# The last product pair of each seven-product group in another order and on other PSUM banks, and the group's first product copied earlier

## The chip, the cores and the metric

The kernel runs on one core of a Trainium2 chip. The metric is the device time of one execution in microseconds (us). Three runs of the kernel before gave 2209.78, 2209.79 and 2210.81 us, median 2209.79.

## What is computed

One inference step of a two-layer backbone (width 1024, 128 context and 512 latent tokens, side by side as 640 columns). The part that matters here is the dense products:

```python
h = RMSNorm(x) * (1 + scale1) + shift1
qkv... = h @ w_in                      # column groups for four mixers
x += gate1 * (sum(gates * up) @ w_o)
h2 = RMSNorm(x) * (1 + scale2) + shift2
a, b = split(h2 @ w_ffn_in)            # w_ffn_in: 1024 x 5632
x += gate2 * ((silu(a) * b) @ w_ffn_out)
```

Everything is float32. Each number is split into a high and a low part, and a product is the sum high*high + high*low + low*high, so three matmuls stand for one.

## The kernel before

Activations lie transposed, 128 channels by 640 token columns, in two halves of 320. A *unit* is a 128x128 piece of weights; `product` (line 755) runs it against both halves, 6 matmuls of 128x320. A *chunk* is one block of 128 output channels: 8 units for an inner width of 1024, 48 matmuls. Two PSUM tensors take the chunks in turn, `lp[0]` for s=0 and `lp[1]` for s=1; each has two banks, `[:, 0]` and `[:, 1]`, one per half. After a chunk DVE or ACT reads the tensor out and counts up `drained[s]`; the next chunk of the same s waits for that. Weights arrive from HBM in `wst[:, s]`, ACT writes their high part to `wr[:, s, 0]` (`weight_hi`), DVE the low part to `wr[:, s, 1]` (`weight_lo`), which counts up `w_lo[s]`.

Part of the in-projection and most of the first feed-forward matrix go another way. A pair of chunks (256 output channels, 1024 inputs, 640 columns) is taken as a 2x2 by 2x2 block product with seven products, P1 to P7, instead of eight (Strassen's scheme in Winograd's form). One product is 12 matmuls of 128x320 (line 1011). There are four groups of such pairs per layer: FAST_IN (6 pairs, 42 products), FAST_A (5 pairs, 35), FAST_B and FAST_C (7 pairs, 49 each), so eight groups in two layers. `ring_order` gives the order: P1 of the first pair, and then for every pair P2, P6, P7, P5, then P1 of the next pair, then P3, P4. In the last pair no P1 stands between P5 and P3.

The seven products use one bank A of their own (P1, then P6, P5 and P3 added on top of it, `bank`) and two shared banks: P2 in `lp[0][:, 1]`, P7 and P4 in `lp[1][:, 1]`. A is `lp[m % 2][:, 0]` for pair m. In between, A is read out: ACT copies it after P1 (`p1_out`) and after P6 (`u2_out`), DVE adds it after P5 (`c22_out`, line 1891), and ACT reads it after P3 (`c12_out`, line 1347). DVE reads P2 (`c11_out`, line 1887) and P4 (`c21_out`, line 1899). P3 waits for `c22_out`, P4 for `p7_out`, P6 for `p1_out`.

The weights of the seven products (operands) are sums and differences of the raw weight blocks. They go through a ring of six places in `wr`: places 0 to 2 lie in `wr[:, 0]`, places 3 to 5 in `wr[:, 1]`. ACT writes the high part (`fast_hi`, line 1315), DVE the low part (`fast_lo`, line 1862, counts up `op_lo`). An operand can be written when the product that used its place before is done: operand i is written around product i-5. One exception is made by `ring_places`: where the last operand of a group would fall on place 0, it takes place 3, so that places 0 to 2 come free for the weights of the next stage:

```python
    places = [i % RING for i in range(n)]
    if places[-1] == 0:
        places[-1] = RING // 2
```

This holds for the groups of 49 products (operand 48, counted from 0), not for those of 42 and 35. The product that had place 3 before is number 45, so operand 48 is written only after it: high part behind product 45 (P7), low part behind product 46 (P5, after the `c22_out` add).

Behind FAST_A, FAST_B and FAST_C come the chunks of `w_ffn_out` (`outward`, eight chunks of 8, 7 and 7 units). Their first weights are loaded into the place of the raw weight blocks, by SP, in this order:

```python
for s in range(2):
    sy.wait_ge(op_lo, nth_op(l, g, FAST[g] - 1, (P3, P4)[s]))
    weight(l, out, src, 0, s)
```

`op_lo` counts operands in the order of the products, so "P3" here means all operands up to and with P3 of the last pair. ACT writes the high part of the first (`out_first_hi`, line 1367) in its step for the third-last product, and DVE the low part (`weight_lo`, line 1623) in its step for the second-last one; both take their steps in the order of the products. Before the first chunk PE waits for `c11_out`, `c12_out` and `c21_out` of the last pair. In layer 1, groups FAST_A and FAST_B, a `modulate_half` (small matmuls, line 1022) stands behind P4 of each of the last four pairs.

At the start of FAST_B and FAST_C the last chunk of the stage before (s=1) has just ended in `lp[1]`, and DVE reads it out in `residual` (line 1643, three instructions); before FAST_A it is the last chunk of the plain feed-forward pairs, read out by DVE at line 2102. P1 of the first pair waits for `drained[0]`, P2 too, and P7 (fourth product) for `drained[1]`. ACT writes operands 3, 4 and 5 there, and then copies P1.

Of the kernel before, what the change touches and what calls it, by code (L numbers as in the profile page):

```python
# [26 lines left out]
P = 128  # L27
DM = 1024
KD = DM // P
# [54 lines left out]
def ring_order(pairs):  # L84

    order = [(0, P1)]
    for m in range(pairs):
        order += [(m, P2), (m, P6), (m, P7), (m, P5)]
        if m + 1 < pairs:
            order.append((m + 1, P1))  # L90
        order += [(m, P3), (m, P4)]
    return order


ORDER = [ring_order(n) for n in FAST]
# [124 lines left out]
def build(nc, xT, ada, adb, win, wgu, wo, wff, wfa, wfb, vec, cond, fgv, cst, rope, dft, bias, ckT, cvt,  # L220
          yT, okT, ovt):
    with ExitStack() as ctx:
# [190 lines left out]
        def pairs_before(l, g, m):  # L413

            return l * FAST0[4] + FAST0[g] + m
# [44 lines left out]
                return H[:, low, HALF_K + k, TH:T]  # L460
            return turned_block(g, {P5: 1, P6: 2, P7: 3, P4: 4}[which], low)[:, k, :]

        def bank(m, which):

            if which in (P2, P7, P4):
                return lp[0 if which == P2 else 1][:, 1, 0:TH]
            return lp[m % 2][:, 0, 0:TH]

        def chunks_of(g, m):

# [279 lines left out]
        def _(pe):  # L750
# [43 lines left out]
            def weights(l, stage, j, s):  # L794
                pe.wait_ge(w_lo[s], 1 + l * PER_SLOT + SLOT0[stage] // 2 + j + 1)

            def fill(l, p, place):

                for n, k in FILL.get((p, place), ()):
                    s = n % 2  # L800
                    if k < KD:
                        if k == 0:
                            weights(l, GATE, n // 2, s)
                            pe.wait_ge(drained[0], gate0(l) + n)
                        mm = product(lp[0], weight_unit(s, k), H, k, k == 0, k == KD - 1)
                        if k == KD - 1:
                            mm.then_inc(lin[0], 1)
                    else:
                        if k == KD:
# [161 lines left out]
            def fast_product(l, g, i):  # L971

                m, which = ORDER[g][i]
                n = pairs_before(l, g, m)
                pe.wait_ge(op_lo, nth_op(l, g, m, which))
                if which == P1:
                    if m >= 2:
                        pe.wait_ge(c12_out, n - 1)
                    else:
                        pe.wait_ge(drained[m], 1 + l * PER_DR + D0[AHEAD[g]])  # L980
                if which == P2:
                    if m:
                        pe.wait_ge(c11_out, n)
                    else:
                        pe.wait_ge(drained[0], 1 + l * PER_DR + D0[AHEAD[g]])
                if which == P7:
                    if m:
                        pe.wait_ge(c21_out, n)
                    else:
                        pe.wait_ge(drained[1], 1 + l * PER_DR + D0[AHEAD[g]])  # L990
                new_blocks = g <= FAST_A and m == 0
                if which == P6:
                    pe.wait_ge(p1_out, n + 1)
                    if new_blocks:
                        pe.wait_ge(t_lo, turned_set(l, g) + 1)
                if which == P7 and new_blocks:
                    pe.wait_ge(t_lo, turned_set(l, g) + 2)
                if which == P5:
                    pe.wait_ge(u2_out, n + 1)
                    if new_blocks:  # L1000
                        pe.wait_ge(t_lo, turned_set(l, g) + 4)
                if which == P3:
                    pe.wait_ge(c22_out, n + 1)
                if which == P4:
                    pe.wait_ge(p7_out, n + 1)
                    if new_blocks:
                        pe.wait_ge(t_lo, turned_set(l, g) + 3)
                fresh = which in (P1, P2, P7)
                for k in range(HALF_K):
                    for j, (wi, ai) in enumerate(((0, 0), (0, 1), (1, 0))):  # L1010
                        mm = pe.matmul(bank(m, which), operand(g, i, wi)[:, k * P:(k + 1) * P], passing(g, which, ai, k),  # L1011
                                       start=fresh and k == 0 and j == 0, stop=k == HALF_K - 1 and j == 2,
                                       skip_group_check=not fresh)
                mm.then_inc(prod, 1)
# [12 lines left out]
            for l in range(L):  # L1027
# [65 lines left out]
                for i, (m, which) in enumerate(ORDER[FAST_IN]):  # L1093
                    fast_product(l, FAST_IN, i)
                    c0, c1 = chunks_of(FAST_IN, m)
                    if which == P2 and m:
                        turn_chunk(c0 - 1)
                    if which == P7 and turn_at(l, c0) is not None:
                        turn_of(c0, turn_at(l, c0))()
                    if which == P4:  # L1100
                        turn_chunk(c0)
                        if c1 < 4 * len(groups_in(l)):
                            quad_in(0)
                            modulate(ss[0], four(sm), c1 // 2 % 2)
# [4 lines left out]
                for c in range(2):  # L1109
# [9 lines left out]
                for out_of in (c11_out, c12_out, c21_out):  # L1119
                    pe.wait_ge(out_of, pairs_before(l, FAST_IN, FAST[FAST_IN]))  # L1120
                fill(l, 0, "f")


# [51 lines left out]
                for g, inner in zip(FF_GROUPS, (S_GA, S_GB, S_GC)):  # L1175
# [10 lines left out]

                    def outward(j, ready=None):
                        for s in range(2):
                            weights(l, out, j, s)
                            chunk(l, out, j, s, G_by_half, range(UNITS[out]), ready=None if s else ready)  # L1190

                    pe.wait_ge(c11_out, pairs_before(l, g, FAST[g]))
                    pe.wait_ge(c12_out, pairs_before(l, g, FAST[g]))
                    pe.wait_ge(c21_out, pairs_before(l, g, FAST[g]))
                    outward(0, inner)
                    with pe.Fori(1, KD // 2 - 1) as j:
                        outward(j)
# [9 lines left out]
        def _(act):  # L1207
# [93 lines left out]
            def fast_hi(l, g, i):  # L1301
# [12 lines left out]
                    act.wait_ge(w_sum, 4 * n + {P5: 1, P7: 2, P6: 3, P3: 4}[which])  # L1314
                act.activation(operand(g, i, 0), source(m, which), ACT.Copy).then_inc(op_hi, 1)  # L1315

            def fast_step(l, g, i):

                m, which = ORDER[g][i]
                n = pairs_before(l, g, m)  # L1320
                A, t1, inner = bank(m, P1), tmp[:, 1, :], g != FAST_IN
                a, b = [product_to(g, m, part) for part in range(2)]
                act.wait_ge(prod, OPS * pairs_before(l, g, 0) + i + 1)
                if which == P1:
                    if n:
                        act.wait_ge(c11_out, n)
                    if g == FAST_A and m == 0:
                        act.wait_ge(split, l * PER_SPL + SP0[S_GA] + 2)
                    act.activation(t1[:, 0:TH], A, ACT.Copy).then_inc(p1_out, 1)
                if which == P6:  # L1330
                    if n:
                        act.wait_ge(c21_out, n)
# [1 line left out]
                if which == P7:  # L1334
                    if inner:
                        act.wait_ge(hid, hid_before(l, g, m))
                    elif turned_before(l, g, m, 1) is not None:
                        act.wait_ge(turned, turned_before(l, g, m, 1))
                    elif chunks_of(g, m)[1] == IN_A + NV_TM:
                        act.wait_ge(op_lo, nth_op(l, g, m, P5))  # L1340
                    act.activation(b[:, TH:T], bank(m, P7), ACT.Copy).then_inc(p7_out, 1)
# [72 lines left out]
            for l in range(L):  # L1414
# [21 lines left out]
                for c in range(2 * PLAIN):  # L1436
# [13 lines left out]
                    if c == 2 * PLAIN - 2:  # L1450
                        for o in range(RING // 2):
                            fast_hi(l, FAST_IN, o)
                for o in range(RING // 2, RING):
                    fast_hi(l, FAST_IN, o)
                for i, (m, which) in enumerate(ORDER[FAST_IN]):
                    fast_step(l, FAST_IN, i)
# [93 lines left out]
                for g in FF_GROUPS:  # L1550
                    out = AHEAD[g]
                    if g > FAST_A:
                        for o in range(RING // 2):
                            fast_hi(l, g, o)
                    for o in range(RING // 2, RING):
                        fast_hi(l, g, o)
                    for i in range(OPS * FAST[g]):
                        fast_step(l, g, i)
# [17 lines left out]
        def _(ve):  # L1576
# [297 lines left out]
            def fast_step(l, g, i):  # L1874
# [5 lines left out]
                if which == P2:  # L1880
# [6 lines left out]
                    ve.tensor_tensor(a[:, 0:TH], tmp[:, 1, 0:TH], bank(m, P2), ALU.add).then_inc(c11_out, 1)  # L1887
                if which == P5:
                    ve.wait_ge(prod, first + i + 1)
                    ve.wait_ge(p7_out, n + 1)  # L1890
                    ve.tensor_tensor(b[:, TH:T], b[:, TH:T], bank(m, P5), ALU.add).then_inc(c22_out, 1)  # L1891
                if which == P4:
                    ve.wait_ge(u2_out, n + 1)
                    ve.wait_ge(prod, first + i + 1)
# [4 lines left out]
                    ve.tensor_tensor(b[:, 0:TH], tmp[:, 1, TH:T], bank(m, P4), ALU.add).then_inc(c21_out, 1)  # L1899
# [370 lines left out]
```

## Time and profile before

| | |
|---|---|
| three runs, median | 2209.79 us |
| profiled execution, time | 2210.49 us |
| its span, first to last instruction | 2208.7 us |
| PE busy | 2143.6 us, 97% of the span |
| DVE busy, ACT busy | 1310.0 us (59%), 900.9 us (41%) |
| matmuls of the seven-product groups (line 1011) | 4200 (2256 + 1368 + 288 + 144 + 96 + 48) |
| mean granted TensorE clock | 0.991 |
| HBM | 101 GB/s over the span |

The profiled execution takes 2210.49 us, 1.8 us more than its span, and lies 0.7 us above the median. Times in the rows below are microseconds from the start of the span. In a timeline row the first number is the start, the second the length of the merged piece, `x12` the number of instructions in it; the bracket gives the engine's idle time before it and what ended it. A piece of matmuls is some 0.15 us longer than the distance to the next piece, because the last matmul overlaps the next one.

### The profile page before, as it was taken

Reading aid. Unit: us, or ns where it says so; the run is one execution under the profiler, and the core shown is the slowest. Engines: PE = TensorE matmul, PEld = TensorE weight load, DVE = VectorE, ACT = ScalarE, POOL = GpSimd, SP = SyncE. Lnnn points to the kernel's source line nnn. Section 1 sums busy time; section 2 is a strip of 40 time slices with the busy share of each in tenths; the row PEclk is TensorE's granted clock in tenths of the full one; section 3 lists DMA queues with packets and bytes.
Section 4 is the critical chain, followed back from the end, with each engine's and each line's share of the span. In section 5 each row is a group of like instructions: output and inputs, shape, how many; then the busy total and the mean of one; then the engine's idle time right before and its main releaser. Section 6 shows DMA issues by size and latency. Waiting matters only on the chain. (4 is left out here: it accounts for less than half of the span.)

```text
span 2208.7 us, 38208 instructions
## 1 busy us (share of the span) xinstructions
PE 2143.6 (97%) x15247; PEld 2018.2 (91%) x15247; DVE 1310.0 (59%) x2493; ACT 900.9 (41%) x1574; POOL 0.2 (0%) x4
## 2 busy tenths in 40 slices
PE   8999999999999999999999999999999999999997
PEld 6998887888998999999989988888899899999997
DVE  5665656665447737558456565566644575474764
ACT  4533444443326415325344334444433364252441
POOL 0000000000000000000000000000000000000000
PEclk9999999999999999999989999999999999999999
DMA  8633321112341422322444233111124232222222
GB/s 295 226 134 109 117 77 49 49 49 72 100 148 61 152 89 92 127 89 77 153 172 161 91 124 118 57 49 49 49 89 156 66 96 68 86 77 72 92 72 81
DMA packets 70774, 225.81 MB, mean 102 GB/s; under 512 B 6992, under 2 KB 13776, under 8 KB 70480
## 3 DMA queue, kind: packets, MB, share of 16 engines
q1 hardware_dynamic: 70608, 223.50, 30.2%
q8 instruction: 116, 1.90, 0.3%
q14 instruction: 50, 0.41, 0.1%
HBM read 215.48 MB, written 6.55 MB: 101 GB/s over the span
## 5 line engine op out<-in xcount | busy, mean ns | idle before, releaser
L755 PE MATMUL lp<-H,wr 128*128 128x320 f32 x4800 | 769.2, 314 | 11.3 <-DVE H L1601 5.1
L755 PEld LDWEIGHTS lp<-H,wr 128*128 128x128 f32 x4800 | 712.4, 189 | 38.2 <-issue 25.5
L1011 PE MATMUL lp<-H,wr 128*128 128x320 f32 x2256 | 350.7, 310 | 5.4 <-DVE tmp L1891 4.0
L1011 PEld LDWEIGHTS lp<-H,wr 128*128 128x128 f32 x2256 | 334.2, 188 | 12.2 <-issue 11.4
L755 PEld LDWEIGHTS lp<-G,wr 128*128 128x128 f32 x2112 | 309.8, 188 | 5.4 <-issue 5.4
L755 PE MATMUL lp<-G,wr 128*128 128x320 f32 x2112 | 311.5, 309 | 3.2 <-issue 3.2
L1229 ACT ACTIVATE wr<-wst 128x1280 fp32r<-128x1280 f32 (+2 forms) x136 | 153.5, 1129 | 179.0 <-PE lp L755 178.3
L1623 DVE TENSOR_TENSOR wr<-wst,wr 128x1280 fp32r<-128x1280 f32 (+2 forms) x152 | 198.4, 1306 | 41.7 <-ACT wr L1229 36.1
L1011 PE MATMUL lp<-TT,wr 128*128 128x320 f32 x1368 | 213.1, 308 | 2.1 <-issue 2.1
L1315 ACT ACTIVATE wr<-wst 128x512 fp32r<-128x512 f32 x256 | 159.6, 627 | 127.4 <-PE lp L1011 75.3
L1011 PEld LDWEIGHTS lp<-TT,wr 128*128 128x128 f32 x1368 | 203.7, 188 | 2.5 <-issue 2.5
L1643 DVE SCALAR_TENSOR_TENSOR x<-lp,mod,x 128x128 f32 (+3 forms) x192 | 72.6, 434 | 201.5 <-PE lp L755 201.5
L1862 DVE TENSOR_TENSOR wr<-wst,wr 128x512 fp32r<-128x512 f32 x256 | 173.7, 685 | 9.1 <-ACT wr L1315 8.9
L755 PE MATMUL lp<-BR,wr 128*128 128x320 f32 x960 | 161.3, 313 | 1.8 <-DVE tmp L1680 1.8
L755 PEld LDWEIGHTS lp<-BR,wr 128*128 128x128 f32 x960 | 143.2, 188 | 8.1 <-issue 3.8
L1271 ACT ACTIVATE prob<-ss,st 128x640 f32<-128x640 f32 (+1 forms) x88 | 59.7, 679 | 132.3 <-DVE st L1722 130.9
L1271 ACT ACTIVATE prob<-sp,st 128x640 f32<-128x640 f32 (+3 forms) x72 | 51.4, 714 | 130.6 <-DVE st L1718 119.7
L1250 ACT ACTIVATE tmp<-lp,vc 128x640 f32<-128x640 f32 x64 | 50.7, 792 | 120.9 <-PE lp L755 120.9
L1283 ACT ACTIVATE pts<-ss 128x640 f32<-128x640 f32 (+3 forms) x120 | 64.4, 570 | 65.2 <-PE ss L912 43.0
L1721 DVE TENSOR_REDUCE st<-ss 128x1 f32<-128x640 f32 (+1 forms) x88 | 59.4, 675 | 50.4 <-PE ss L885 37.8
L1518 ACT ACTIVATE tmp<-x 128x640 f32 (+1 forms) x32 | 23.6, 739 | 159.9 <-DVE x L1643 159.9
L1680 DVE SCALAR_TENSOR_TENSOR tmp<-tmp,lp 128x640 f32<-128x640 f32 x48 | 39.2, 816 | 69.6 <-PE lp L755 69.3
(200 smaller groups left out, 2125.4 us busy)
## 6 DMA issues: line engine op xcount, KB each, us to landing
wst<-wgu SPq DMA_DIRECT2D x64, 640.0 KB, 3.9
wst<-wff SPq DMA_DIRECT2D x72, 512.0 KB, 3.6
sm<-adb SPq DMA_DIRECT2D x13, 2048.0 KB, 8.5
wst<-win SPq DMA_DIRECT2D x30, 512.0 KB, 4.5
wst<-wfb SPq DMA_DIRECT2D x32, 448.0 KB, 3.3
bt<-bias SPq DMA_DIRECT2D x32, 320.0 KB, 3.3
adae<-adb SPq DMA_DIRECT2D x8, 1024.0 KB, 15.0
wst<-wo SPq DMA_DIRECT2D x16, 512.0 KB, 3.7
```

Of the source, the lines that this page charges most:

```text
L755: mm = pe.matmul(out[:, h, 0:TH], w[wi], act[:, ai, k, h * TH:(h + 1) * TH], start=first and i == 0, stop=last and i == 2)
L1011: mm = pe.matmul(bank(m, which), operand(g, i, wi)[:, k * P:(k + 1) * P], passing(g, which, ai, k), start=fresh and k == 0 and j == 0, sto ...
L1229: act.activation(wr[:, s, 0, 0:w], wst[:, s, 0:w], ACT.Copy).then_inc(w_hi[s], 1)
L1250: act.activation(halves(tmp[:, 2 + n % 2, :]), lp[0][:, :, 0:TH], ACT.Tanh, bias=vc[:, i:i + 1], scale=0.5).then_inc(drained[0], 1)
L1271: act.activation(prob[:, u, lo:hi], src, ACT.Exp, bias=nm[:, q:q + 1], scale=SC_DIFF if kind == "df" else 1.0, accum_out=rs[:, q:q + 1]).t ...
L1283: act.activation(pts[:, f % 2, lo:KEYS], sflat[u][:, lo:KEYS], ACT.Copy).then_inc(pt_out, 1)
L1315: act.activation(operand(g, i, 0), source(m, which), ACT.Copy).then_inc(op_hi, 1)
L1623: ve.tensor_tensor(wr[:, s, 1, 0:w], wst[:, s, 0:w], wr[:, s, 0, 0:w].bitcast(F32), ALU.subtract).then_inc(w_lo[s], 1)
L1643: m = ve.scalar_tensor_tensor(out=x[:, k, a:b], in0=lp[s][:, h, a - h * TH:b - h * TH], scalar=mod[:, gate + 2 * j + s, c:c + 1], in1=x[:, ...
L1680: ve.scalar_tensor_tensor(out=halves(mg[:, kd, :] if first else tmp[:, 1, :]), in0=gate, scalar=1.0, in1=up, op0=ALU.add, op1=ALU.mult).th ...
L1721: own.step(ve.tensor_reduce(mx, S[:, at_:at_ + KEYS - lo], AX.X, ALU.max))
L1862: ve.tensor_tensor(operand(g, i, 1), source(m, which), operand(g, i, 0).bitcast(F32), ALU.subtract).then_inc(op_lo, 1)
```

## The change

The order of the last pair of every group becomes P2, P6, P7, P5, P4, P3. Bank A of pair m becomes `lp[(FAST[g] - m) % 2][:, 0]`, so that the last pair always has A in `lp[1]`; for the groups of 35 and 49 products this turns all banks A round, and the first pair has A in `lp[1]` as well. P1 of the first two pairs waits for `drained` of its own bank. The wait ahead of the next stage is split: the chunk in `lp[0]` waits for `c11_out` of the last pair and `c12_out` of the pair before, the chunk in `lp[1]` for `c12_out` and `c21_out` of the last pair. ACT copies the group's first product behind operand 3, ahead of operands 4 and 5. In FAST_IN the transposes of the last pair's first chunk (`turn_chunk`) move behind P3, which is now the last product. `ring_places`, SP's code, and the steps of `out_first_hi` and `weight_lo` stay as they are.

```diff
@@ ring_order
         order += [(m, P2), (m, P6), (m, P7), (m, P5)]
         if m + 1 < pairs:
-            order.append((m + 1, P1))
-        order += [(m, P3), (m, P4)]
-    return order
+            order += [(m + 1, P1), (m, P3), (m, P4)]
+    return order + [(pairs - 1, P4), (pairs - 1, P3)]
...
+        def first_bank(g, m):
+            return (FAST[g] - m) % 2
...
             if which in (P2, P7, P4):
                 return lp[0 if which == P2 else 1][:, 1, 0:TH]
-            return lp[m % 2][:, 0, 0:TH]
+            return lp[first_bank(g, m)][:, 0, 0:TH]
@@ PE
+            def first_bank_free(l, g):
+                pe.wait_ge(c11_out, pairs_before(l, g, FAST[g]))
+                pe.wait_ge(c12_out, pairs_before(l, g, FAST[g] - 1))
+            def second_bank_free(l, g):
+                pe.wait_ge(c12_out, pairs_before(l, g, FAST[g]))
+                pe.wait_ge(c21_out, pairs_before(l, g, FAST[g]))
...
-                        pe.wait_ge(drained[m], 1 + l * PER_DR + D0[AHEAD[g]])
+                        pe.wait_ge(drained[first_bank(g, m)], 1 + l * PER_DR + D0[AHEAD[g]])
...
-                    if which == P4:
+                    if which == (P3 if m == FAST[FAST_IN] - 1 else P4):
                         turn_chunk(c0)
...
                         for s in range(2):
+                            if isinstance(j, int) and j == 0:
+                                (second_bank_free if s else first_bank_free)(l, g)
                             weights(l, out, j, s)
...
-                    pe.wait_ge(c11_out, pairs_before(l, g, FAST[g]))
-                    pe.wait_ge(c12_out, pairs_before(l, g, FAST[g]))
-                    pe.wait_ge(c21_out, pairs_before(l, g, FAST[g]))
                     outward(0, inner)
@@ ACT
-                for o in range(RING // 2, RING):
+                fast_hi(l, FAST_IN, RING // 2)
+                first_product_out(l, FAST_IN, 0)
+                for o in range(RING // 2 + 1, RING):
                     fast_hi(l, FAST_IN, o)
...
-                    for o in range(RING // 2, RING):
+                    fast_hi(l, g, RING // 2)
+                    first_product_out(l, g, 0)
+                    for o in range(RING // 2 + 1, RING):
                         fast_hi(l, g, o)
```

`first_product_out` is the copy that stood in ACT's step for P1, with the same waits. The three places below show how the instructions move. In the rows `lp0` and `lp1` are the two PSUM tensors, `H` and `TT` the activation blocks, `G` the inner activations of the feed-forward part; the bracket names the semaphores that the instruction waits for.

PE, end of FAST_B in layer 1, from P5 to the first chunk behind the group, before:

```order
L1011 MATMUL lp0<-H_52,wr_89 128x320 [waits u2_out,op_lo]
L1011 MATMUL lp0<-H_52,wr_89 128x320 x11
L1011 MATMUL lp0<-H_52,wr_89 128x320 [waits c22_out,op_lo]
L1011 MATMUL lp0<-H_52,wr_89 128x320 x11
L1011 MATMUL lp1<-TT_56,wr_89 128x320 [waits p7_out,op_lo]
L1011 MATMUL lp1<-TT_56,wr_89 128x320 x11
L1022 MATMUL ss0<-sm2_57,cds_91 32x256 [waits ld_h]
L1022 MATMUL ss0<-sm2_57,cds_91 32x256 x7
L755 MATMUL lp0<-G_55,wr_89 128x320 [waits w_lo0,drained0,c21_out,split,c12_out,c11_out]
```

The same place in the change:

```order
L1026 MATMUL lp1<-H_52,wr_89 128x320 [waits u2_out,op_lo]
L1026 MATMUL lp1<-H_52,wr_89 128x320 x11
L1026 MATMUL lp1<-TT_56,wr_89 128x320 [waits p7_out,op_lo]
L1026 MATMUL lp1<-TT_56,wr_89 128x320 x11
L1037 MATMUL ss0<-sm2_57,cds_91 32x256 [waits ld_h]
L1037 MATMUL ss0<-sm2_57,cds_91 32x256 x7
L1026 MATMUL lp1<-H_52,wr_89 128x320 [waits c22_out,op_lo]
L1026 MATMUL lp1<-H_52,wr_89 128x320 x11
L758 MATMUL lp0<-G_55,wr_89 128x320 [waits drained0,w_lo0,split,c12_out,c11_out]
```

P4 and the small matmuls now stand between P5 and P3, and the first chunk no longer waits for `c21_out`.

DVE, the same end of FAST_B, before (line 1891 reads P5, 1862 writes operand 48, 1623 the low part of the next stage's first weights, 1899 reads P4):

```order
L1891 TENSOR_TENSOR tmp_87<-tmp_87,lp0 128x320 [waits p7_out,prod]
L1862 TENSOR_TENSOR wr_89<-wst_88,wr_89 128x512 [waits op_hi]
L1623 TENSOR_TENSOR wr_89<-wst_88,wr_89 128x896 [waits w_hi0]
L1899 TENSOR_TENSOR tmp_87<-tmp_87,lp1 128x320 [waits prod,u2_out]
L1919 TENSOR_TENSOR tmp_87<-tmp_87 128x640 [waits c22_out,c21_out,split,c12_out,c11_silu]
```

In the change:

```order
L1915 TENSOR_TENSOR tmp_87<-tmp_87,lp1 128x320 [waits p7_out,prod]
L1886 TENSOR_TENSOR wr_89<-wst_88,wr_89 128x512 [waits op_hi]
L1923 TENSOR_TENSOR tmp_87<-tmp_87,lp1 128x320 [waits prod,u2_out]
L1647 TENSOR_TENSOR wr_89<-wst_88,wr_89 128x896 [waits w_hi0]
L1943 TENSOR_TENSOR tmp_87<-tmp_87 128x640 [waits c22_out,c21_out,split,c12_out,c11_silu]
```

The weights' low part now stands behind the read of P4. Operand 48, in the second row, was P4's and is now P3's.

PE, start of FAST_B in layer 1, the last chunk before it and P1, P2 and P6, before:

```order
L755 MATMUL lp1<-G_55,wr_89 128x320 x47
L1011 MATMUL lp0<-H_52,wr_89 128x320 [waits drained0,op_lo]
L1011 MATMUL lp0<-H_52,wr_89 128x320 x11
L1011 MATMUL lp0<-H_52,wr_89 128x320 [waits drained0,op_lo]
L1011 MATMUL lp0<-H_52,wr_89 128x320 x11
L1011 MATMUL lp0<-TT_56,wr_89 128x320 [waits p1_out,op_lo]
```

In the change:

```order
L758 MATMUL lp1<-G_55,wr_89 128x320 x47
L1026 MATMUL lp1<-H_52,wr_89 128x320 [waits drained1,op_lo]
L1026 MATMUL lp1<-H_52,wr_89 128x320 x11
L1026 MATMUL lp0<-H_52,wr_89 128x320 [waits drained0,op_lo]
L1026 MATMUL lp0<-H_52,wr_89 128x320 x11
L1026 MATMUL lp1<-TT_56,wr_89 128x320 [waits p1_out,op_lo]
```

P1 now goes to the tensor that the chunk directly ahead of it has filled, and waits for `drained1`.

## Rows read from the trace of the kernel before

**Rows 1.** Waits of PE: whom it waited for, total us, times, longest us.

```profile
PE lp L1011 <- DVE tmp L1891: 4.0, 6, 0.7
PE lp L1011 <- DVE qk L1891: 1.3, 2, 0.7
PE lp L755 <- issue: 3.2, 4, 0.8
```

**Rows 2.** Timeline, end of FAST_B in layer 2.

```profile
1996.53 20.37 SPq L553 DMA_DIRECT2D wst<-wfb  x5
...
2000.42 1.92 PE L1011 MATMUL lp<-H,wr 128*128 128x320 f32 x12
...
2002.38 0.95 ACT L1367 ACTIVATE wr<-wst 128x896 fp32r<-128x896 f32 x1 [0.80 <-PE lp L1011]
...
2002.79 0.68 DVE L1862 TENSOR_TENSOR wr<-wst,wr 128x512 fp32r<-128x512 f32 x1
...
2003.02 2.00 PE L1011 MATMUL lp<-H,wr 128*128 128x320 f32 x12 [0.67 <-DVE tmp L1891]
2003.39 1.09 DVE L1623 TENSOR_TENSOR wr<-wst,wr 128x896 fp32r<-128x896 f32 x1
...
2007.58 12.70 PE L755 MATMUL lp<-G,wr 128*128 128x320 f32 x85 [0.80 <-issue]
```

**Rows 3.** Timeline, start of FAST_B in layer 2.

```profile
1919.46 3.68 PE L1011 MATMUL lp<-H,wr 128*128 128x320 f32 x24
...
1919.67 1.13 DVE L1643 SCALAR_TENSOR_TENSOR x<-lp,mod,x 128x128 f32<-128x128 f32 x3 [1.20 <-PE lp L755]
```

**Rows 4.** DMA issues near Rows 2: two loads, KB each, us to landing.

```profile
wst<-wfb SPq DMA_DIRECT2D x1, 448.0 KB, 3.4
...
wst<-wfb SPq DMA_DIRECT2D x1, 448.0 KB, 4.1
```

**Rows 5.** Timeline, end of FAST_A in layer 2, ends of FAST_A and FAST_B in layer 1.

```profile
1859.05 1.23 DVE L1623 TENSOR_TENSOR wr<-wst,wr 128x1024 fp32r<-128x1024 f32 x1 [0.69 <-ACT wr L1367]
...
1862.37 0.49 DVE L1899 TENSOR_TENSOR tmp<-tmp,lp 128x320 f32<-128x320 f32 x1 [2.10 <-PE lp L1011]
...
777.95 1.07 PE L1022 MATMUL ss<-sm,cds 128*32 128x256 f32 x16
...
923.12 0.68 DVE L1862 TENSOR_TENSOR wr<-wst,wr 128x512 fp32r<-128x512 f32 x1
...
928.04 12.15 PE L755 MATMUL lp<-G,wr 128*128 128x320 f32 x81
```

**Rows 6.** Timeline, start of FAST_A in layer 2.

```profile
1798.25 3.77 PE L1011 MATMUL lp<-H,wr 128*128 128x320 f32 x24
1798.31 0.82 DVE L2102 TENSOR_TENSOR tmp<-lp,tmp 128x640 f32<-128x640 f32 x1 [2.85 <-PE lp L755]
...
1800.98 0.61 ACT L1315 ACTIVATE wr<-wst 128x512 fp32r<-128x512 f32 x1
...
1802.54 0.41 ACT L1329 ACTIVATE tmp<-lp 128x320 f32<-128x320 f32 x1
...
1803.05 3.75 PE L1011 MATMUL lp<-TT,wr 128*128 128x320 f32 x24 [1.03 <-issue]
```

**Rows 7.** PE's longest idle times early in the mixers of each layer, and the block behind the first (timeline).

```profile
198.18 0.49 PE L898 MATMUL ss<-qk 64*128 64x128 f32 x4 [2.21 <-DVE ofm L1769]
198.60 3.10 PE L755 MATMUL lp<-H,wr 128*128 128x320 f32 x12
...
1286.92 0.49 PE L898 MATMUL ss<-qk 64*128 64x128 f32 x4 [1.58 <-DVE ofm L1769]
```

**Rows 8.** Stretches of PE: length, busy (matmuls), granted clock, DMA share, GB/s.

```profile
199.00:199.50 0.50, 0.50 (x5) 0.69 0.00 0
...
202.50:203.00 0.50, 0.50 (x5) 0.90 0.00 0
...
2002.00:2008.00 6.00, 4.52 (x30) 1.00 0.46 148
```

More of the change, by code:

```diff
@@ L461, in passing, with bank @@
             return turned_block(g, {P5: 1, P6: 2, P7: 3, P4: 4}[which], low)[:, k, :]
-        def bank(m, which):
+        def first_bank(g, m):
+            return (FAST[g] - m) % 2
+        def bank(g, m, which):
             if which in (P2, P7, P4):
                 return lp[0 if which == P2 else 1][:, 1, 0:TH]
-            return lp[m % 2][:, 0, 0:TH]
+            return lp[first_bank(g, m)][:, 0, 0:TH]
         def chunks_of(g, m):
@@ L808, in fill @@
                     else:
+                        if (n, k) == (0, KD):
+                            second_bank_free(l, FAST_IN)
                         if k == KD:
@@ L1010, in fast_product @@
                     for j, (wi, ai) in enumerate(((0, 0), (0, 1), (1, 0))):
-                        mm = pe.matmul(bank(m, which), operand(g, i, wi)[:, k * P:(k + 1) * P], passing(g, which, ai, k),
+                        mm = pe.matmul(bank(g, m, which), operand(g, i, wi)[:, k * P:(k + 1) * P], passing(g, which, ai, k),
                                        start=fresh and k == 0 and j == 0, stop=k == HALF_K - 1 and j == 2,
@@ L1118, in _ @@
                     mm.then_inc(f1, 1)
-                for out_of in (c11_out, c12_out, c21_out):
-                    pe.wait_ge(out_of, pairs_before(l, FAST_IN, FAST[FAST_IN]))
+                first_bank_free(l, FAST_IN)
                 fill(l, 0, "f")
@@ L1315, in fast_hi, with first_product_out @@
                 act.activation(operand(g, i, 0), source(m, which), ACT.Copy).then_inc(op_hi, 1)
+            def first_product_out(l, g, m):
+                n = pairs_before(l, g, m)
+                act.wait_ge(prod, OPS * pairs_before(l, g, 0) + PLACE[g][m, P1] + 1)
+                if n:
+                    act.wait_ge(c11_out, n)
+                if g == FAST_A and m == 0:
+                    act.wait_ge(split, l * PER_SPL + SP0[S_GA] + 2)
+                act.activation(tmp[:, 1, 0:TH], bank(g, m, P1), ACT.Copy).then_inc(p1_out, 1)
             def fast_step(l, g, i):
@@ L1320, in fast_step @@
                 n = pairs_before(l, g, m)
-                A, t1, inner = bank(m, P1), tmp[:, 1, :], g != FAST_IN
+                A, t1, inner = bank(g, m, P1), tmp[:, 1, :], g != FAST_IN
                 a, b = [product_to(g, m, part) for part in range(2)]
@@ L1324, in fast_step @@
                 if which == P1:
[L1325 to L1329, printed above, removed]
+                    if m:
+                        first_product_out(l, g, m)
                 if which == P6:
@@ L1340, in fast_step @@
                         act.wait_ge(op_lo, nth_op(l, g, m, P5))
-                    act.activation(b[:, TH:T], bank(m, P7), ACT.Copy).then_inc(p7_out, 1)
+                    act.activation(b[:, TH:T], bank(g, m, P7), ACT.Copy).then_inc(p7_out, 1)
                 if which == P3:
@@ L1886, in fast_step @@
                     ve.wait_ge(prod, first + i + 1)
-                    ve.tensor_tensor(a[:, 0:TH], tmp[:, 1, 0:TH], bank(m, P2), ALU.add).then_inc(c11_out, 1)
+                    ve.tensor_tensor(a[:, 0:TH], tmp[:, 1, 0:TH], bank(g, m, P2), ALU.add).then_inc(c11_out, 1)
                 if which == P5:
@@ L1890, in fast_step @@
                     ve.wait_ge(p7_out, n + 1)
-                    ve.tensor_tensor(b[:, TH:T], b[:, TH:T], bank(m, P5), ALU.add).then_inc(c22_out, 1)
+                    ve.tensor_tensor(b[:, TH:T], b[:, TH:T], bank(g, m, P5), ALU.add).then_inc(c22_out, 1)
                 if which == P4:
@@ L1898, in fast_step @@
                         ve.wait_ge(turned, turned_before(l, g, m, 1))
-                    ve.tensor_tensor(b[:, 0:TH], tmp[:, 1, TH:T], bank(m, P4), ALU.add).then_inc(c21_out, 1)
+                    ve.tensor_tensor(b[:, 0:TH], tmp[:, 1, TH:T], bank(g, m, P4), ALU.add).then_inc(c21_out, 1)
                 for o in range(RING - 1, OPS * FAST[g]):
```

## The prediction

> **What bounds the kernel now.** I read the list of what PE waited for first, then the timeline of each kind of group end and group start, then the DMA issues, and last the stretches with the granted clock. PE is the bound, so the change can only act through PE's gaps. There are two kinds at a group's end [rows 1]: P3 of the last pair waits for the DVE read of P5, 0.67 us in all eight groups (six under `tmp`, two under `qk`), and the first outward chunk starts 0.80 us late behind P4 in four of the six feed-forward groups. [Rows 2] show one such end, FAST_B of layer 2: P5 starts at 2000.42, P3 follows its 0.67 us gap, and the outward chunk starts at 2007.58 behind 0.80 us. The change is aimed at both.
>
> A gap costs a little more than it shows. Two products in a row take 3.68 us [rows 3] and one takes 1.92 us [rows 2], so a product costs 1.76 us when the next follows at once; the other 0.16 us overlaps. With it the two gaps cost 0.83 and 0.96 us.
>
> **Ends of FAST_B and FAST_C (four).** Both gaps go, and something worse comes. P3's operand is now operand 48, whose low part DVE finished at 2002.79 + 0.68 = 2003.47 in [rows 2]; P5 and its read don't move, so neither does this time. SP lets the first outward weights (s=0) go only when this operand is done. Before it asked for operand 47, and issued that load at 1996.53, 6.9 us earlier. From there all is serial:
>
> - load: 3.4 us to landing in the near row, 4.1 for one behind another [rows 4]. I take 3.4, because this load goes first; s=1 now follows it at once. It lands at 2006.9.
> - ACT's high part: 0.95 us [rows 2] and 0.05 to notice, done at 2007.9.
> - DVE's low part: 1.09 us [rows 2] and 0.05, done at 2009.0. The read of P4 that now stands ahead of it is long over.
> - PE starts 0.2 us behind a DVE result (the estimate comes from [rows 5], where the read of P4 ends at 1862.86 and the 0.8 us gap behind it ends 0.2 us later): 2009.2.
>
> Before, PE started at 2007.58, so this end costs +1.64 us. PE itself is done early: P5 at 2000.42, P4, P3 and the next start at 2000.42 + 3 x 1.76 = 2005.7, some 3.3 us idle. FAST_B of layer 1 has small matmuls (1.07 us, [rows 5]) in that hole, but not on the serial path: operand 48 done at 923.80, start 5.74 us later at 929.54 against 928.04, +1.50 us. Sum of the four: 3 x 1.64 + 1.50 = **+6.4 us**.
>
> The Trainium skill, "DMA: Bandwidth & Descriptors" (Latency and other measured facts; Where 436 GB/s comes from), prices a load at some 2 us fixed plus its bytes at 436 GB/s, an estimate of 3.05 us for 448 KB. By it the four ends would cost 1.4 us less. The measured 3.4 us stands.
>
> What else waits there: ACT sits in the wait for this load and reads P3 late, so the last inner block is made late. The chain (DVE product, ACT copy, DVE low part, each some 0.8 us) starts when DVE is free at 2009.0 and ends near 2011.6; the chunk wants that block in its last seventh, 5.3 us after 2009.2. It is hidden, with 2.9 us to spare.
>
> **Ends of FAST_A (two).** Its last operand falls on place 4, written six products before its use, so the load is not late. But DVE now reads P4 before it writes the low part. In layer 2 the start is P4's end + 0.1 + 0.49 + 1.23 + 0.2, less 0.08 overlap = 1.94 us [rows 5], of which P3 covers 1.60. The gap is 0.34 instead of 0.96, and the 0.83 goes: -1.45 us. In layer 1 the small matmuls already cover the second gap, only 0.83 goes. Sum **-2.3 us**.
>
> **Ends of FAST_IN (two).** 0.83 us goes, but the transposes of the last pair now stand behind P3 and wait for ACT's copy of it: 0.04 + 0.41 (its length in [rows 6]) + 0.2, and 0.16 overlap, 0.81. Sum **0**.
>
> **Starts of FAST_B and FAST_C (four).** P1 now goes into the tensor that the chunk just ahead has filled, and waits for DVE to read it. In [rows 3] DVE reads it in 1919.67 to 1920.80, while P1 has been running since 1919.46. Now P1 starts at 1921.00: +1.54 us each, **+6.2 us**. The earlier copy of P1 gains nothing here: in [rows 1] no wait of P6 is listed for these groups.
>
> **Starts of FAST_A (two).** P1 waits for the read at line 2102, 1798.31 to 1799.13 [rows 6], so it starts at 1799.33 instead of 1798.25. But P6 stood 1.03 us behind ACT's copy of P1, which began at 1802.54 after three operands. Now the copy stands behind the first of them (done at 1801.59), P1 ends before that, and the copy is over at 1802.0; P6 comes at 1799.33 + 2 x 1.76 = 1802.85 instead of 1803.05. Sum **-0.4 us**. Operands 4 and 5 come later by one copy on ACT, 0.4 us, and by P1's wait; the products that use them are at least four products away, so this costs nothing.
>
> Bare sum: 6.4 - 2.3 + 0 + 6.2 - 0.4 = **+9.9 us**.
>
> **The clock.** In each layer's mixers one longer idle time of PE stands: 2.21 us before 198.18, 1.58 us before 1286.92 [rows 7]. Behind each the granted clock fell from 2.4 to 1.2 GHz, in the first case from about 199.1 to 202.6 [rows 8], and 12 matmuls took 3.10 us. The two short gaps of an old group end left it at full (2002 to 2008, [rows 8]). The new holes of 3.3 us (2.3 in FAST_B of layer 1) are longer than both that pulled it down, and dense work follows. 3.5 us at half speed lose 1.75 us; part of it may pass while PE still waits, so I take 1.6 us for each of four ends, between 0 and 2.6 (a second stretch): **+6.4 us**.
>
> Sum: +16.3 us. Against the profiled execution this is 2210.49 + 16.3 = 2226.8; the median of the runs is 0.7 lower, so I predict **2226 us**, +0.74%. About 0.2%, 4.4 us, is what a measurement of this kernel can tell from no change.
>
> **The rivals.**
>
> *The clock holds.* Then only the bare sum is left, 2219.7. For it: the 2.21 and 1.58 us stand next to small matmuls, and need not have pulled it down alone. Against it: they are longer by half. Chance 0.2. The Trainium skill, "TensorE: Matmul & The Clock Gate" (HAM oscillation), warns only of idle gaps longer than any that I expect here; by it this rival would hold, but its rule disagrees with [rows 7, 8], where 1.58 us was enough.
>
> *The clock falls at the group starts too.* The new hole there is about 1.4 us, between the 0.80 that did nothing and the 1.58 that did. Four more falls at 1.7 us: 2226 + 6.8 = 2233. Chance 0.18.
>
> *Not slower: the load is in time.* It decides at one point: to be hidden, the first weights must land by about 2003.4 on the clock of [rows 2], that is, be issued by 2000.0. That would hold if P3's operand were written on an early ring place, as it is in FAST_A. Then the four ends would save both gaps less some 0.25 us (3 x 1.54 + 0.83 = 5.4), and with the starts the sum is 6.2 - 0.4 - 2.3 - 5.4 = -1.9: 2208. Against it speak `ring_places` and SP's unchanged wait. Chance 0.04.
>
> **How the numbers follow.** Forecast 0.58, clock holds 0.2, clock falls at the starts too 0.18, load in time 0.04. The first three are slower by over 0.2%, the last lies within it; of the first three I leave 0.01 for a mistake that ends faster: faster 0.01, same 0.04, slower 0.95. The unknown prices: the load between 3.0 and 4.1 us (-1.6 to +2.8 over four ends), the clock between 0 and 2.6 us per end. The range goes from the rival without a fall and a slightly faster load, 2217.5, to the one with falls at the starts, 2233.
>
> **What would show it.** In the profile after, the 0.67 us waits of PE for the read of P5 are gone in all groups. At four outward starts PE waits some 3.3 us (one: 2.3) for the DVE low part of the weights (`wr`), ACT's high part there waits for the DMA, and SP issues the first load of `wfb` behind operand 48. At four group starts PE waits some 1.4 us for `x`, the residual. The granted clock shows half behind the outward starts. FAST_A ends 1.4 us sooner in layer 2, and P6 no longer waits at its start. It is wrong if the load is issued before P5 is done, if PE does not wait at P1, or if the clock stays at full throughout.

## The result and the profile after

The change makes the kernel slower: 2226.99 us, median of 4 runs (2225.59 to 2229.88), against 2210.30 us for the kernel before, median of 4 runs beside them (2209.78 to 2212.10). The ratio is 1.0077, 95% interval 1.0065 to 1.0089. Forecast were 2226 us and a range from 2217.5 to 2233. The profiled execution of the change took 2225.59 us against 2210.49, 15.1 us more, and that difference is taken apart here. In the code of the change the products stand in line 1026, the chunks in 758, the reads of P5 and P4 in 1915 and 1923, the operands' low part in 1886, the weights' high and low part in 1387 and 1647, the residual in 1667, the copy of P1 in 1338.

From the profile page: the engines' busy time, two groups of matmuls, and the loads of `wfb`.

```profile
PE 2149.5 (97%) x15247; PEld 2023.1 (91%) x15247; DVE 1308.8 (59%) x2493; ACT 899.8 (40%) x1574; POOL 0.2 (0%) x4
...
L1026 PE MATMUL lp<-H,wr 128*128 128x320 f32 x2256 | 350.5, 310 | 6.8 <-DVE x L1667 5.3
...
L758 PE MATMUL lp<-G,wr 128*128 128x320 f32 x2112 | 317.4, 312 | 12.9 <-issue 12.9
...
wst<-wfb SPq DMA_DIRECT2D x32, 448.0 KB, 3.4
```

The work is the same, but PE is busy 5.9 us longer (2143.6 before), mostly because part of it runs at half clock (below). The other 9 us are idle time. What PE waited for, total us, times, longest us:

```profile
PE lp L758 <- issue: 12.9, 5, 3.6
PE lp L1026 <- DVE x L1667: 5.3, 4, 1.3
...
PE lp L1026 <- DVE tmp L2126: 1.6, 2, 0.8
...
PE ss L1105 <- issue: 1.2, 2, 0.6
```

The waits for the read of P5, 4.0 and 1.3 us in [rows 1], are gone in all eight groups. The outward chunks' wait, 3.2 us in four places in [rows 1], is now 12.9 us in five, with 3.6 for the longest. The second row is new: four group starts wait 1.3 us each for the residual. So is the third: P1 at the two FAST_A starts, where the wait of P6 (1.03 us, [rows 6]) is gone. The last is the wait of the transposes (line 1105), which takes the place of P5's read in FAST_IN.

The end of FAST_B in layer 2, the place of [rows 2] (timeline: start, length, engine, line, operation; the bracket is the idle time before and what ended it):

```profile
2007.31 1.92 PE L1026 MATMUL lp<-H,wr 128*128 128x320 f32 x12
2009.07 1.92 PE L1026 MATMUL lp<-TT,wr 128*128 128x320 f32 x12
2009.27 0.49 DVE L1915 TENSOR_TENSOR tmp<-tmp,lp 128x320 f32<-128x320 f32 x1 [2.55 <-PE lp L1026]
2009.67 0.68 DVE L1886 TENSOR_TENSOR wr<-wst,wr 128x512 fp32r<-128x512 f32 x1
2010.39 22.73 SPq L556 DMA_DIRECT2D wst<-wfb  x6
2010.83 1.92 PE L1026 MATMUL lp<-H,wr 128*128 128x320 f32 x12
...
2013.90 0.95 ACT L1387 ACTIVATE wr<-wst 128x896 fp32r<-128x896 f32 x1 [5.43 <-issue]
2014.88 1.09 DVE L1647 TENSOR_TENSOR wr<-wst,wr 128x896 fp32r<-128x896 f32 x1 [3.29 <-ACT wr L1387]
2016.22 17.05 PE L758 MATMUL lp<-G,wr 128*128 128x320 f32 x105 [3.46 <-issue]
```

Read it as one serial line: operand 48 is done at 2009.67 + 0.68 = 2010.35, SP issues the load at 2010.39, ACT starts 3.51 us later, then DVE, then PE at 2016.22. The three products run through without a gap (2007.31, 2009.07, 2010.83), and PE is idle for 3.46 us behind them. From P5 to the outward chunk it is 8.91 us, against 7.16 in [rows 2]. The profile puts PE's wait down to "issue", not to the weights' low part, whose end at 2015.97 is 0.25 us before PE's start; that this part ends the wait is shown by experiment 1, which moves it, and in experiment 3 the profile names it.

The granted clock there (stretch, length, busy and matmuls, clock, DMA share, GB/s):

```profile
2012.00:2014.00 2.00, 0.75 (x6) 1.00 0.91 355
...
2016.00:2017.00 1.00, 0.78 (x3) 0.50 0.00 0
2017.00:2018.00 1.00, 1.00 (x6) 0.50 0.69 97
2018.00:2019.00 1.00, 1.00 (x5) 0.50 0.89 362
2019.00:2020.00 1.00, 1.00 (x7) 0.83 0.09 16
2020.00:2022.00 2.00, 2.00 (x16) 1.00 0.58 161
```

From 2016 to 2019.3 the clock is at half, 1.2 GHz; full speed, 2.4 GHz, is back before 2020. In the timeline the first 12 matmuls, from 2016.22, take 3.42 us, while 43 from 2019.77 on take 6.47. Read in finer stretches, it is 3.4 us at half behind each of the four ends (also from about 930.4, 1073.8 and 2159.2), which costs 1.7 us each; in FAST_B of layer 2 the first 0.3 us of it pass while PE still waits.

Two other ends, FAST_C in layer 2 (its P5 and outward chunk) and FAST_A in layer 2 (P5 and outward chunk):

```profile
2149.51 1.92 PE L1026 MATMUL lp<-H,wr 128*128 128x320 f32 x12
...
2158.35 11.89 PE L758 MATMUL lp<-G,wr 128*128 128x320 f32 x69 [3.40 <-issue]
```

```profile
1862.78 1.92 PE L1026 MATMUL lp<-H,wr 128*128 128x320 f32 x12
...
1868.40 3.76 PE L758 MATMUL lp<-G,wr 128*128 128x320 f32 x24 [0.19 <-issue]
```

FAST_C takes 8.84 us from P5 to its chunk (7.15 before); FAST_A, whose operand is written early, takes 5.62 (7.15 before).

The start of FAST_B in layer 2, the place of [rows 3]:

```profile
1925.00 1.14 DVE L1667 SCALAR_TENSOR_TENSOR x<-lp,mod,x 128x128 f32<-128x128 f32 x3 [1.20 <-PE lp L758]
...
1926.28 3.75 PE L1026 MATMUL lp<-H,wr 128*128 128x320 f32 x24 [1.32 <-DVE x L1667]
```

Before, P1 started 0.21 us ahead of the residual; now it starts 1.28 us behind the residual's start, so 1.49 us are lost.

The start of FAST_A in layer 2, the place of [rows 6]: the small matmuls ahead of the group, P1 (with P2), and P5 (with the two products behind it):

```profile
1805.21 0.38 PE L844 MATMUL ss<-con,grow 128*128 128x128 f32 x2
1806.38 3.76 PE L1026 MATMUL lp<-H,wr 128*128 128x320 f32 x24 [0.79 <-DVE tmp L2126]
...
1813.49 5.45 PE L1026 MATMUL lp<-H,wr 128*128 128x320 f32 x36
```

P1 now waits 0.79 us, but P6 no longer waits: from the small matmuls to P5 it is 8.28 us, against 8.53 before (1798.11 to 1806.64).

### The profile page after: what moved, and what is told of

It is laid out like the page before. It is cut to its first block and busy times, and to the rows that moved or that the text cites. A ratio compares the mean times of both kernels' runs of the same rounds, so it can differ in the third digit from the quotient of the medians.

```text
span 2223.7 us, 38204 instructions
## 1 busy us (share of the span) xinstructions
PE 2149.5 (97%) x15247; PEld 2023.1 (91%) x15247; DVE 1308.8 (59%) x2493; ACT 899.8 (40%) x1574; POOL 0.2 (0%) x4
## 5 line engine op out<-in xcount | busy, mean ns | idle before, releaser
L758 PE MATMUL lp<-G,wr 128*128 128x320 f32 x2112 | 317.4, 312 | 12.9 <-issue 12.9
L758 PEld LDWEIGHTS lp<-G,wr 128*128 128x128 f32 x2112 | 315.8, 191 | 14.5 <-issue 14.5
```

The lines of the kernel that those rows point to most:

```text
L758: mm = pe.matmul(out[:, h, 0:TH], w[wi], act[:, ai, k, h * TH:(h + 1) * TH], start=first and i == 0, stop=last and i == 2)
```

## The experiments

Each was timed with the kernel before beside it: 2210.30 us beside the first four (19 runs), 2210.68 us beside the last two (21 runs). Line numbers differ from the change's by up to four; those of experiment 5 are the kernel before's, or up to eleven more.

**1. The operand earlier.** The change, with the last two operands of a group of 49 on other places of the ring, so that operand 48 is written well before P5. Banks, order and SP's code stay.

```diff
-        places[-1] = RING // 2
+        places[-2:] = [0, RING - 1]
...
+HI_STEP = [[max(steps[:i + 1]) for i in range(len(steps))] for steps in HI_STEP]
```

> The changed kernel with other ring places for the last two operands of FAST_B and FAST_C: P4's on place 0, P3's on place 5, so that P3's operand is written three products earlier (in the step of the last pair's P2) and the load of the first outward weights goes off before P5. Theory (the load behind operand 48 is what PE waits for at these four ends, and the hole pulls the clock down): the high part now waits for P4 instead, so the start comes about 2.3 us behind P4's end, 0.6 us of idle time is left in three ends and none in FAST_B of layer 1. Against the changed kernel 3 x 2.9 + 2.6 = 11.3 us less from the holes and 6.8 us less from four clock falls that no longer come: about 2209 us, no different from the kernel before. Rival A (the hole has another cause, such as DVE's read of P4 that now stands ahead of the low part, or P3's own late start): nothing changes, 2227. Rival B (the load is the cause, the clock is not part of the price): 2227 - 11.3 = 2216.

Measured: 2209.09 us (11 runs, 2207.60 to 2212.36), ratio to before 0.9997 (0.9988 to 1.0006), 17.9 us under the change. The same end of FAST_B in layer 2:

```profile
1996.09 11.64 SPq L557 DMA_DIRECT2D wst<-wfb  x4
...
1997.60 1.92 PE L1027 MATMUL lp<-H,wr 128*128 128x320 f32 x12
...
2001.40 0.95 ACT L1388 ACTIVATE wr<-wst 128x896 fp32r<-128x896 f32 x1 [3.16 <-PE lp L1027]
...
2002.39 1.09 DVE L1648 TENSOR_TENSOR wr<-wst,wr 128x896 fp32r<-128x896 f32 x1 [0.51 <-ACT wr L1388]
...
2003.69 8.60 PE L759 MATMUL lp<-G,wr 128*128 128x320 f32 x57 [0.65 <-ACT tmp L1368]
```

The load now goes 1.51 us ahead of P5, not 3.08 us behind its start, and P5 to the chunk takes 6.09 us. The other three such ends measure 6.46, 6.08 and 6.13. Together that is 11.0 us less than in the change; with four falls of the clock at 1.7 us, none of which is there now, 17.8 us, against 17.9 measured. So the late load carries the whole loss at the ends, and the falls hang on it. A gap of 0.65 us stays: ACT's high part waits for P4, whose operand lies where these weights go, and the low part ends at 2003.48, 0.21 us before PE starts (the row names the read of P3 by ACT, which ends at about the same time, but by the code this chunk does not wait for it).

**2. The old banks.** The change, with A of pair m in `lp[m % 2]` as before.

```diff
-            return (FAST[g] - m) % 2
+            return m % 2
...
-                pe.wait_ge(c12_out, pairs_before(l, g, FAST[g] - 1))
+                pe.wait_ge(c12_out, pairs_before(l, g, FAST[g] - (FAST[g] + 1) % 2))
```

> The changed kernel with bank A of pair m back in lp[m % 2], so that P1 of FAST_B and FAST_C no longer goes into the tensor that the chunk ahead has filled; the waits ahead of the next stage are fitted to it. Order, ring and early copy stay. Theory (P1 waits for the residual read): the 1.3 us waits of PE for x go at four starts, 1.5 us each; FAST_A's starts gain 0.7 us each and its ends lose some 0.5 to 0.8 us, because P3 now has to be read before the next chunk; the four late loads stay as they are. About 6 us less than the changed kernel, 2221 us, with the four holes of 3.5 us and the four clock falls unchanged. Rival (P1 would wait for something else there, an operand or the weights): 2227, and a wait of 1.3 us at P1 under another name.

Measured: 2221.29 us (5 runs, 2220.20 to 2223.29), ratio 1.0050 (1.0037 to 1.0064), 5.7 us under the change. The largest wait of PE for the chunks, and the start of FAST_B in layer 2:

```profile
PE lp L758 <- issue: 13.0, 5, 3.4
```

```profile
1923.31 3.68 PE L1026 MATMUL lp<-H,wr 128*128 128x320 f32 x24
```

The starts wait no more, and the wait for the residual is gone from the table; the four ends wait nearly as in the change (12.4 us of the 13.0, against 12.8), and the clock falls behind all four. The four starts give back 4 x 1.49 = 6.0 us. At the ends of FAST_A the turned banks were worth something: with the old ones the chunk waits for P3's read, as in layer 2,

```profile
1866.91 8.30 PE L758 MATMUL lp<-G,wr 128*128 128x320 f32 x55 [0.62 <-ACT tmp L1367]
```

and P5 to the chunk is 7.25 us in layer 1 and 6.06 in layer 2, against 6.48 and 5.62, 1.2 us in all. At the two FAST_A starts P1's wait goes, but P5 waits instead for the low part of its operand, so that only 0.06 us each are left (8.22 us from the small matmuls to P5, against 8.28); the four late ends are 0.4 us shorter in all. That makes 5.3 us, against 5.7 measured. Turned banks for FAST_A alone were not tried.

**3. The hole filled.** The change, with five matmuls (three in FAST_B of layer 1) ahead of the first outward chunk of FAST_B and FAST_C, into a bank that is free and whose content the chunk then overwrites. The profile lists each of them as two instructions.

```diff
+                                if not s and g > FAST_A:
+                                    for _ in range(3 if l == 0 and g == FAST_B else 5):
+                                        pe.matmul(lp[0][:, 0, 0:2 * P], ones, con[:, 0:2 * P], start=True, stop=True)
```

> The changed kernel with five matmuls of 128x256 of constants (three in FAST_B of layer 1) put into the hole ahead of the first outward chunk of FAST_B and FAST_C; they write a part of lp[0] that the chunk then overwrites, and their results are not used. The load is as late as before and nothing else moves. Theory (each hole lets the clock fall to 1.2 GHz for 3.4 us, at a price of 1.7 us): the clock stays at 2.4 GHz behind the four ends, the chunks start at the same moment, and the time falls by 6.8 us to about 2220. Rival (the falls cost nothing, because PE waits for something else behind the hole, or the clock falls in any case): 2227 or a little more.

Measured: 2218.84 us (5 runs, 2217.88 to 2220.84), ratio 1.0037 (1.0024 to 1.0051), 8.2 us under the change although PE does more. The end of FAST_B in layer 2, and the clock there:

```profile
2010.89 2.32 PE L1207 MATMUL lp<-con 128*128 128x256 f32 x10
2012.12 0.95 ACT L1390 ACTIVATE wr<-wst 128x896 fp32r<-128x896 f32 x1 [5.36 <-issue]
2013.11 1.09 DVE L1650 TENSOR_TENSOR wr<-wst,wr 128x896 fp32r<-128x896 f32 x1 [3.22 <-ACT wr L1390]
2014.25 9.95 PE L758 MATMUL lp<-G,wr 128*128 128x320 f32 x66 [1.04 <-DVE wr L1650]
```

```profile
2014.00:2016.00 2.00, 1.75 (x12) 1.00 0.30 70
2016.00:2018.00 2.00, 2.00 (x15) 1.00 0.41 160
```

The serial line of load, ACT and DVE is untouched; only PE's idle time is 1.04 us instead of 3.46, and the clock stays at full behind all four ends. This gives the clock's price apart from the wait: four times 1.7 us, and besides it the four ends are shorter by 0.27, 0.28, 0.36 and -0.03 us, mostly because PE starts sooner behind DVE (0.05 us here, 0.25 in the change); together 7.7 us of the 8.2. The two profiled executions lie only 4.8 us apart (2220.84 is the longest of the five runs): this one takes 1.9 us longer up to the small matmuls ahead of FAST_A in layer 1 (711.59 against 709.69), where it holds five stretches at half clock and the change three.

**4. Both mended.** Experiments 1 and 2 together, and the last pair's `modulate_half` (layer 1) moved from behind P4 to behind P3, beside the wait that is left there.

```diff
-                        if which == P4 and l + 1 < L:
+                        if which == (P3 if m == FAST[g] - 1 else P4) and l + 1 < L:
```

> Early operand and old banks together, and the small matmuls behind the last pair's P4 in layer 1 moved behind P3. What is left of the change is the order P5, P4, P3 and the early copy of P1. Theory: neither hole is left; each feed-forward group end costs some 0.8 us for the read of P3 where it cost 0.83 + 0.96 us (0.83 where small matmuls cover the second), so 4 x 1.07 + 2 x 0.92 = 6.1 us less than the kernel before, and 0.9 us less at each of two FAST_A starts: 2210.3 - 7.9 = 2202.4 us. Rival (the two gaps at a group's end are worth less than they show, because the next wait takes their place): 2208 to 2211.

Measured: 2204.26 us (9 runs, 2202.70 to 2206.45), ratio 0.9975 (0.9965 to 0.9985). This is faster than the kernel before by 6.0 us and than the change by 22.7. The ends gave what was expected, 6.1 us; the 1.8 us expected of the copy are not there (experiments 5 and 6 take it apart). The end of FAST_B in layer 2:

```profile
1994.15 1.92 PE L1027 MATMUL lp<-H,wr 128*128 128x320 f32 x12
...
2000.24 5.96 PE L759 MATMUL lp<-G,wr 128*128 128x320 f32 x39 [0.65 <-ACT tmp L1368]
```

**5. The copy alone.** The kernel before, with P1's copy ahead of operand five's store and nothing else.

```diff
-                    for o in range(RING // 2, RING):
+                    fast_hi(l, g, RING // 2)
+                    first_product_out(l, g, 0)
+                    for o in range(RING // 2 + 1, RING):
```

> The kernel before with one part of the change alone: at a pair's first product P1 is copied to tmp ahead of operand five's store; banks, the order of the last pair and the operand ring are those of before. My theory: at the two FAST_A starts the wait of P6 (1.03 us, beside the clock's small change) goes and 0.9 us each is gained, nothing at the other starts, where another wait ended last; about 1.8 us in all, so about 2208.5 us, with the wait of P6 on the copy gone from the table of PE's waits. Rival one: the copy has no part in it and the time stays at 2210.3. Rival two: operand five, now stored later by about 0.45 us, makes P5 late at some start: 2211 or more, with a wait of the products on that store.

Measured: 2209.66 us (11 runs, 2208.90 to 2211.37), ratio 0.9996 (0.9987 to 1.0005): 1.0 us less, which the interval does not tell from nothing. The start of FAST_A in layer 2 (PE), the place of [rows 6]:

```profile
1797.43 0.38 PE L829 MATMUL ss<-con,grow 128*128 128x128 f32 x2
1797.57 3.77 PE L1011 MATMUL lp<-H,wr 128*128 128x320 f32 x24
1801.33 3.76 PE L1011 MATMUL lp<-TT,wr 128*128 128x320 f32 x24
1805.64 5.52 PE L1011 MATMUL lp<-H,wr 128*128 128x320 f32 x36 [0.56 <-DVE wr L1873]
```

P6 waits no more, but the next product but one now stands 0.56 us behind the low part of its operand. From the small matmuls ahead of the group to that product it is 8.21 us against 8.53 in the kernel before (1798.11 to 1806.64): 0.32 us a start, not 0.9. My theory fell here, and the second half of it, that nothing else would wait, is the part that failed. Of rival two the wait came true, P5 behind its operand, but not its time: P5 still starts earlier than before.

**6. The order alone.** Experiment 4 without the early copy.

```diff
-                    fast_hi(l, g, RING // 2)
-                    first_product_out(l, g, 0)
-                    for o in range(RING // 2 + 1, RING):
+                    for o in range(RING // 2, RING):
```

> The best version so far (new order of the last pair, its banks as before, operand 48 one place earlier in the ring, the last pair's modulate behind P3) without the early copy of P1. My theory: parts add up, so it takes 2204.3 us plus what the copy alone is worth, 1.8 us: about 2206, and PE waits at the two FAST_A starts for the copy of P1 again. Rival: the copy is worth nothing beside the new order, since another wait takes its place: 2204.3 us. Rival two: the whole gain of the best version is the copy's and the order's is nothing: 2208.5 us.

Measured: 2204.64 us (11 runs, 2202.91 to 2207.03), ratio 0.9975 (0.9966 to 0.9984). The start of FAST_A in layer 2:

```profile
1800.03 3.75 PE L1027 MATMUL lp<-TT,wr 128*128 128x320 f32 x24 [1.03 <-issue]
```

The wait of P6 is back and the time is that of experiment 4 within its uncertainty; my 2206 had the copy at 1.8 us, and after experiment 5 it is 0.6 for both starts, too little to be told apart. Rival one's time, 2204.3, fits, and experiment 5 shows the wait that takes the place. So the gain is that of the new order with operand 48 written early: in this kernel's six feed-forward ends P5 to the outward chunk is shorter by 1.06, 1.07, 1.06, 0.91, 1.09 and 0.92 us, 6.1 us in all, against 6.0 measured.

## Why the prediction was right, step by step

Measured in the profiled executions, from P5 to the first outward chunk at the ends, and from the small matmuls ahead of the group to P5, the fifth product, at the FAST_A starts:

| step | predicted | measured |
|---|---|---|
| ends of FAST_B and FAST_C (four) | +6.4 | 1.75 + 1.62 + 1.93 + 1.69 = +7.0 |
| ends of FAST_A (two) | -2.3 | -1.53 - 0.80 = -2.3 |
| ends of FAST_IN (two), from P5 to the transposes | 0 | 6.06 against 6.19 and 6.06 against 6.20, -0.3 |
| starts of FAST_B and FAST_C (four) | +6.2 | 4 x 1.49 = +6.0 |
| starts of FAST_A (two) | -0.4 | -0.25 - 0.24 = -0.5 |
| clock falls behind the four ends | +6.4 | 4 x 1.7 = +6.8 |
| sum | +16.3 | +16.7, and 15.1 between the two executions |

**The late load** held in each of its parts. The load was taken at 3.4 us: from issue to ACT's start it is 3.51, and 3.47 to 3.69 over the four ends. The Trainium skill, "DMA: Bandwidth & Descriptors" (Latency and other measured facts; Where 436 GB/s comes from), gave an estimate of 3.05 us; the trace is above it. The 0.2 us behind DVE was 0.21 to 0.25. The largest miss is FAST_C in layer 1, +1.93, where the load takes the 3.69 us and PE's idle time is the longest, 3.64 us. The rival with the load in time, 2208 us, is what experiment 1 nearly makes (2209.09).

**The banks** held too: 1.3 us of idle time at each start, predicted as some 1.4. The clock did not fall there, so the rival of 2233 us falls. But the reason that the prediction weighed, a length between the 0.80 us that did nothing and the 1.58 that did, is not borne out: in the kernel before a fall also follows waits of 0.99 and 1.03 us, in a stretch of small matmuls (timeline, then the granted clock behind it):

```profile
1746.30 1.27 PE L841 MATMUL ss<-con,tmp 128*128 128x1 f32 x10 [0.99 <-ACT tmp L1518]
1748.61 1.14 PE L850 MATMUL ss<-con,st 128*128 128x128 f32 x5 [1.03 <-DVE st L1582]
...
1750.00:1752.00 2.00, 2.00 (x24) 0.50 0.61 227
```

So the length of one wait does not settle it. At the group starts dense matmuls stand on both sides of the 1.3 us; whether that is what kept the clock up was not tried, so the forecast that it holds there came true without its reason being shown.

**The clock** was the step with the widest bounds, and it fell at all four ends, as the forecast had it; the rival of 2219.7 us, in which it holds, is what experiment 3 nearly makes (2218.84, with the sooner starts of PE in it). The rule that the prediction set against it, of the Trainium skill, "TensorE: Matmul & The Clock Gate" (HAM oscillation), warns of long idle gaps only. The gaps of 3.46, 3.40 and 3.64 us are about as long as those that it warns of and do not speak against it; that of FAST_B in layer 1, 2.26 us behind a product, is shorter, and a fall followed it as well. There the measurement decides. That the fall needs the idle time, and not only the late chunk, is shown by experiment 3.

**The copy** is the place where the working was luckier than it was good. For the change it gave -0.4 and -0.5 was measured, because P1's new wait of 0.79 us leaves room for the low part of P5's operand. The prediction held that operands written one copy later cost nothing. That DVE's chain of operands is the next limit was not in it, and experiments 2 and 5 show it: without P1's wait P5 waits some 0.56 us for that operand.

**The difference between 16.7 and 15.1** lies in the mixers, which the change does not touch. From the outward chunk of FAST_C in layer 1 to the small matmuls ahead of FAST_A in layer 2 it is 732.35 us before (1065.76 to 1798.11) and 732.59 after (1072.62 to 1805.21), though the latter begins with the fall behind the FAST_C end, 1.7 us. In the rest of that part the clock is at half for 20.5 us before and for 17.1 after, one fall fewer, worth 1.7 us, which is the difference. (The part ahead of FAST_A in layer 1 is 0.24 us shorter, with three falls in either.) What decides where the clock falls there was not tried.

## What to carry to other kernels

When the order of the last steps is changed, follow what each queue waits for beyond the products: here SP asked for a count of operands that the new order reaches 7.0 us later as seen from P5 (3.08 us behind its start instead of 3.89 ahead), and a hidden load became a serial line of load, ACT and DVE. A wait of a few microseconds in front of dense matmuls costs more than its length when the clock falls behind it (here 1.7 us more), so price it with and without the fall. And a wait that goes is worth only the distance to the next one: 1.03 us of P6's wait was worth 0.32.

## What was not expected of the hardware

The same idle time of PE did not always pull the clock down. In the first layer's mixers PE waits 2.21 us before the small matmuls at 198.18 [rows 7]; after the change it waits 2.20 us at the same place. Two microseconds behind it, in the kernel before and then in the change:

```profile
200.00:202.00 2.00, 2.00 (x11) 0.50 0.00 0
```

```profile
198.22 0.49 PE L913 MATMUL ss<-qk 64*128 64x128 f32 x4 [2.20 <-DVE ofm L1793]
...
200.00:202.00 2.00, 1.29 (x10) 1.00 0.00 0
```

With the same wait there the clock fell in the kernel before and in experiments 2, 3, 5 and 6, and stayed at full in the change and in experiments 1 and 4. Up to there the change and experiments 1, 2 and 3 run the same code. So a fall that one profile shows behind such a wait is not a fixed price, and single profiles differ by a few falls of 1.7 us without any cause in the code.

Also new: PE started 0.05 us behind DVE's result when it had just run the extra matmuls, and 0.25 us behind it after 3.46 us of idle time. The length of the idle time alone is not the cause: in experiment 3 it was 1.04 us, and in experiment 1, after 0.65 us, PE starts 0.21 us behind that result. What makes the difference was not tried.
